# Conditioning beside every second piece in the first layer and every piece in the second; the feed-forward's first products in one matmul of 512 columns and one of 256

## The reference, cut to what matters

```
def swiglu(x, w1, w3, w2):
    return (jax.nn.silu(x @ w1) * (x @ w3)) @ w2        # 1024 -> 2816 -> 1024
...
for i in range(DEPTH):                                  # two layers
    x = layer_norm(DEEPNORM_ALPHA * x + mix, ln1_g[i], ln1_b[i])
    x = layer_norm(DEEPNORM_ALPHA * x + swiglu(x, ffn_w1[i], ffn_w3[i], ffn_w2[i]), ln2_g[i], ln2_b[i])
    x = x + jax.nn.sigmoid(x @ ple_w_gate[i] + ple_b_gate[i]) * (p[i] @ ple_w_proj[i])
...
mod = jax.nn.silu(c) @ w_ada[l] + b_ada[l]              # second block: 1024 -> 6144, once
```

## Time and profile before

| | |
|---|---|
| median of 3 runs | 1837.02 us (1832.55 to 1837.19) |
| the profiled execution | 1836.56 us |
| its span, first to last instruction | 1835.0 us |
| PE busy | 1768.0 us (96%) |
| DVE busy | 1245.4 us (68%) |
| ACT busy | 902.1 us (49%) |
| read from memory | 172 GB/s over the span |

### The profile page before, as it was taken

One profiled execution on the slowest core, in us unless ns is written; L12 is line 12 of the kernel. 1 busy time (PEld: TensorE's weight loads), 2 busy tenths in 40 slices (PEclk: granted clock), 3 DMA queues, 4 the chain that ended last, 5 costly groups with the idle time before them and its releaser, 6 DMA issues.

```text
span 1835.0 us, 32435 instructions
## 1 busy us (share of the span) xinstructions
PE 1768.0 (96%) x11628; PEld 1593.5 (87%) x11628; DVE 1245.4 (68%) x2324; ACT 902.1 (49%) x1585; POOL 206.8 (11%) x148
## 2 busy tenths in 40 slices
PE   9999999799999999998989999999999999999997
PEld 8769998678879997796779999999998998888886
DVE  5467767776768666856656884777886556666666
ACT  5634443355544433646335545777774444333333
POOL 1010000001110000021112788000000000000000
PEclk9999999899999999998989999999999999999999
DMA  7424658745536666344214455444345555555553
GB/s 241 173 98 155 251 181 298 249 168 173 168 113 226 233 235 223 127 154 138 75 64 152 159 184 182 144 144 141 139 139 172 183 184 182 192 186 190 188 188 133
DMA packets 86359, 317.60 MB, mean 173 GB/s; under 512 B 9632, under 2 KB 9904, under 8 KB 85488
## 3 DMA queue, kind: packets, MB, share of 16 engines
q1 hardware_dynamic: 77328, 279.48, 43.7%
q10 hardware_dynamic: 7200, 25.45, 4.0%
q0 software_dynamic: 1728, 11.25, 1.7%
HBM read 315.08 MB, written 1.05 MB: 172 GB/s over the span
## 4 chain that ended last, share of the span: by engine, by line
PE 70%; DVE 4%; ACT 2%; issue 1%; POOL 0%; ACTq 0%; DVEq 0%; POOLq 0%
PE bank L244 21%; PE bank L246 21%; PE bank L245 21%; PE bank L2202 3%; ACT wh L192 1%; DVE wl L199 1%; PE bank L489 1%; PE bank L524 1%; PE bank L559 0%; PE bank L2046 0%; PE bank L523 0%; PE bank L490 0%; DVE ss_s L527 0%; DVE xl L368 0%; PE bank L342 0%
## 5 line engine op out<-in xcount | busy, mean ns | idle before, releaser
L192 ACT ACTIVATE wh<-ring 128x1024 fp32r<-128x1024 f32 x529 | 559.3, 1059 | 776.0 <-PE bank L246 708.4
L199 DVE TENSOR_TENSOR wl<-ring,wh 128x1024 fp32r<-128x1024 f32 x479 | 586.4, 1226 | 440.0 <-ACT wh L192 440.0
L244 PE MATMUL bank<-xh,wh 128*128 128x256 f32 x2072 | 597.2, 288 | 6.8 <-DVE xl L368 6.6
L246 PE MATMUL bank<-xh,wl 128*128 128x256 f32 x2072 | 589.4, 284 | 0.0
L245 PE MATMUL bank<-xl,wh 128*128 128x256 f32 x2072 | 589.1, 284 | 0.0
L244 PEld LDWEIGHTS bank<-xh,wh 128*128 128x128 f32 x2072 | 400.5, 193 | 10.4 <-issue 7.7
L245 PEld LDWEIGHTS bank<-xl,wh 128*128 128x128 f32 x2072 | 400.0, 193 | 1.1
L246 PEld LDWEIGHTS bank<-xh,wl 128*128 128x128 f32 x2072 | 399.8, 193 | 0.0
L244 PE MATMUL bank<-wh,wa_high 128*128 128x512 f32 x512 | 202.4, 395 | 2.1 <-DVE weighted L2221 1.4
L246 PE MATMUL bank<-wh,wa_low 128*128 128x512 f32 x512 | 201.9, 394 | 0.0
L245 PE MATMUL bank<-wl,wa_high 128*128 128x512 f32 x512 | 201.9, 394 | 0.0
(11 more groups left out here) (431 smaller groups left out, 2235.3 us busy)
## 6 DMA issues: line engine op xcount, KB each, us to landing
ring<-in_stream SPq DMA_DIRECT2D x529, 512.0 KB, 3.3
ada<-in_w_ada ACTq DMA_DIRECT2D x48, 512.0 KB, 4.5
rows<-in_rows POOLq DMA_DIRECT2D x1, 2560.0 KB, 12.5
rows<-in_rows POOLq DMA_DIRECT2D x2, 1024.0 KB, 5.2
con<-in_early POOLq DMA_DIRECT2D x1, 1374.0 KB, 15.2
x_feature_major<-in_x_fm SPq DMA_DIRECT2D x4, 256.0 KB, 5.2
x<-in_x_tm POOLq DMA_DIRECT2D x1, 1024.0 KB, 5.6
weighted<-in_subkeys POOLq DMA_DIRECT2D x1, 1024.0 KB, 5.3
```

The source lines that it names most:

```text
L192: C.activation(wh[q % AHEAD][:, :], ring[slot][:, :], ACT.Copy).then_inc(s_high, 1)
L199: low.tensor_tensor(wl[q % AHEAD][:, :], ring[slot][:, :], wh[q % AHEAD][:, :], ALU.subtract).then_inc(s_low, 1)
L244: T.matmul(o, left[0], right[0], start=start, stop=False, skip_group_check=True)
L246: return T.matmul(o, left[1], right[0], start=False, stop=stop, skip_group_check=True)
```

## The change

`xh` and `xl` become halves of one tensor `xs`, in which both halves of a k stand side by side, 2 x 256 columns. A first product's step over k is then one matmul that streams all 512 columns past `wh` (sums of the high half in a bank's first 256 columns, of the low half in the other 256) and one that streams 256 past `wl`. The two halves of the bank must be added afterwards: an ACT copy and a DVE add for `ga` and the same for `gb`. `ada["every"]` behind the first products is 2 in layer 0 and 1 in layer 1, where it was 1 in both.

```diff
-    xh = sb(base, "xh", [P, KD, S], F32R)
-    xl = sb(base, "xl", [P, KD, S], F32R)
+    xs = sb(base, "xs", [P, KD, 2, S], F32R)
+    xh, xl = xs[:, :, 0, :], xs[:, :, 1, :]
...
+        def wide(g, k, h, l):
+            ks = slice(k * P, (k + 1) * P)
+            T.matmul(g[:, :], h[:, ks], xs[:, k, :, :].rearrange("p a t -> p (a t)"), start=k == 0, stop=False,
+                     skip_group_check=True)
+            return T.matmul(g[:, 0:S], l[:, ks], xh[:, k, :], start=False, stop=k == KD - 1, skip_group_check=True)
...
-                        last = mm3(g[:, 0:S], (h[:, k * P:(k + 1) * P], l[:, k * P:(k + 1) * P]),
-                                   (xh[:, k, :], xl[:, k, :]), k == 0, k == KD - 1)
+                        last = wide(g, k, h, l)
...
-                    C.activation(sg[u % 3][:, :], ga[:, 0:S], ACT.Silu).then_inc(s_silu, 1)
-            V.wait_ge(s_used, s + (q + 2))
-            V.wait_ge(s_silu, n3 + (u + 1))
-            V.tensor_tensor(hf[u % 3][:, :], sg[u % 3][:, :], gb[:, 0:S], ALU.mult).then_inc(s_gate, 1)
+                    C.activation(sg[u % 3][:, :], ga[:, S:2 * S], ACT.Copy).then_inc(s_silu, 1)
+                    V.wait_ge(s_silu, n9 + (3 * u + 1))
+                    V.tensor_tensor(sg[u % 3][:, :], ga[:, 0:S], sg[u % 3][:, :], ALU.add).then_inc(s_gate, 1)
+            C.wait_ge(s_gate, n15 + (5 * u + 1))
+            C.activation(sg[u % 3][:, :], sg[u % 3][:, :], ACT.Silu).then_inc(s_silu, 1)
+            C.wait_ge(s_used, s + (q + 2))
+            if i is not None or u >= 3:
+                C.wait_ge(s_gate, n15 + 5 * (u - 3) + 5)
+            C.activation(hf[u % 3][:, :], gb[:, S:2 * S], ACT.Copy).then_inc(s_silu, 1)
+            V.wait_ge(s_silu, n9 + (3 * u + 3))
+            V.tensor_tensor(hf[u % 3][:, :], gb[:, 0:S], hf[u % 3][:, :], ALU.add).then_inc(s_gate, 1)
+            V.wait_ge(s_gate, n15 + (5 * u + 2))
+            V.tensor_tensor(hf[u % 3][:, :], sg[u % 3][:, :], hf[u % 3][:, :], ALU.mult).then_inc(s_gate, 1)
...
-        ada["every"] = 1
+        ada["every"] = 2 - layer
         y = project((hh, hl), KF, sums[0:2], need=gated_in)
```

More of the change, by code:

```diff
@@ L1076, in products_side_by_side @@
                     h, l = wh[(q0 + piece) % AHEAD], wl[(q0 + piece) % AHEAD]
-                    last = mm3(bank[3 * piece][:, 0:S], (h[:, k * P:(k + 1) * P], l[:, k * P:(k + 1) * P]),
-                               (xh[:, k, :], xl[:, k, :]), k == 0, k == KD - 1)
+                    last = wide(bank[3 * piece], k, h, l)
                     if k == KD - 1:
@@ L1084, in tile @@
             n3 = 0 if i is None else i * 3
+            n9 = 0 if i is None else i * 9
+            n15 = 0 if i is None else i * 15
             s = 0 if i is None else i * BODY
@@ L1091, in tile @@
                     if i is not None or u >= 3:
-                        T.wait_ge(s_gate, 3 * n3 + 3 * (u - 3) + 1 if i is not None else 3 * (u - 3) + 1)
+                        T.wait_ge(s_gate, n15 + 5 * (u - 3) + 2)
                 def products(h, l, g=g):
@@ L1108, in tile @@
                     if i is not None or u >= 3:
-                        C.wait_ge(s_gate, 3 * n3 + 3 * (u - 3) + 1)
-                    C.activation(sg[u % 3][:, :], ga[:, 0:S], ACT.Silu).then_inc(s_silu, 1)
-            V.wait_ge(s_used, s + (q + 2))
-            V.wait_ge(s_silu, n3 + (u + 1))
-            V.tensor_tensor(hf[u % 3][:, :], sg[u % 3][:, :], gb[:, 0:S], ALU.mult).then_inc(s_gate, 1)
-            V.wait_ge(s_gate, 3 * n3 + (3 * u + 1))
+                        C.wait_ge(s_gate, n15 + 5 * (u - 3) + 3)
+                    C.activation(sg[u % 3][:, :], ga[:, S:2 * S], ACT.Copy).then_inc(s_silu, 1)
[11 more added lines that the diff above has]
+            V.tensor_tensor(hf[u % 3][:, :], sg[u % 3][:, :], hf[u % 3][:, :], ALU.mult).then_inc(s_gate, 1)
+            V.wait_ge(s_gate, n15 + (5 * u + 3))
             row = u if i is None else bass.ds(n3 + u, 1)
@@ L1118, in tile @@
             V.tensor_copy(hrow, hf[u % 3][:, :]).then_inc(s_gate, 1)
-            V.wait_ge(s_gate, 3 * n3 + (3 * u + 2))
+            V.wait_ge(s_gate, n15 + (5 * u + 4))
             V.tensor_tensor(lrow, hf[u % 3][:, :], hrow, ALU.subtract).then_inc(s_gate, 1)
@@ L1155, in ffn @@
         sums = [bank[6], bank[7], bank[1], bank[4]]
-        gated_in = lambda k: pe.wait((s_gate, 3 * max(k + 1, KF - 2)))
-        ada["every"] = 1
+        gated_in = lambda k: pe.wait((s_gate, 5 * max(k + 1, KF - 2)))
+        ada["every"] = 2 - layer
         y = project((hh, hl), KF, sums[0:2], need=gated_in)
@@ L1705, in opened @@
         pe.wait(zr)
-        T.matmul(bank[4][:, :], zrow[:, :], xh[0:1, 0:2, :].rearrange("p a t -> p (a t)"), start=True, stop=False,
+        T.matmul(bank[4][:, :], zrow[:, :], xs[0:1, 0, :, :].rearrange("p a t -> p (a t)"), start=True, stop=False,
                  skip_group_check=True)
```

1 line of the change is left out of this document (removed).

## The result

| | before | after |
|---|---|---|
| median | 1836.78 us (1832.55 to 1838.79, 8 runs) | 1842.39 us (1834.25 to 1848.32, 8 runs) |
| profiled execution | 1836.56 us | 1840.76 us |

The ratio is 1.0033, 95% interval 1.0021 to 1.0045: slower by 0.33%. The forecast was no change, 1836 us; the time lies within its range.

A forecast was written before the change was run, and what follows sets the result against it. PE, busy for 96% of the span, was taken as the bound. The profiled 1836.6 us, less 9.2 (first products), less 14.4 (layer 0), plus 23.1 (layer 1), gave 1836.1 us; range for 8 in 10: 1828 to 1845.

The forecast's parts named there:

- The first products: PE's k-steps in both layers' first products: 0.360 to 0.347 us over 704 steps, 9.2 us gained, at the least 4.2.
- The sum: All terms added to the profiled execution: 1836.6 less 9.2, less 14.4, plus 23.1, giving 1836.1 us.
- DVE and ACT: First products' extra copies and adds: costed at nothing, ACT having room and three pieces of lead covering DVE's tight tiles.
- Layer 0: Behind layer 0's first products, half the conditioning steps: 6.15, 4.9 and 3.3 us gained, together 14.4.
- Layer 1: Behind layer 1's first products, 11 more conditioning steps left for later: 1.3 + 20.1 + 1.7 = 23.1 us lost (21 to 29).
- the row: Eight leftover conditioning steps after layer 1's residual, ahead of the low half PE needs: eighth starts at 15.8 us, ends at 17.0.
- the 1.3 us of loss ahead of it: Layer 1's first `project`, a step at each of 11 steps: PE runs dry after 40.7 us where pieces take 39.4.
- The clock's part: PE coming back slow after layer 1's idle stretch: 1.7 us added (none, or 3.4).
- The rival that layer 1 keeps its lead: Layer 1's row begins over 3 us earlier with three pieces ready, PE idles some 13 us for 20.1: 1828; chance 0.22.
- DVE as the bound: Rival in the first products: waits make a loop tile 5.9 us on DVE, 44 tiles lose 15 us: 1851; chance 0.12.
- Halving: Rival that layer 0's halved steps still fall behind, half of the 14.4 us stays: 1843; chance 0.16 with the 512-column pace.
- The second part of that rival: First products' 512-column pace is 0.234 us or more, giving 1841; chance 0.16 together with layer 0's halving.

The follow-up runs named there:

- e1: The changed kernel with the conditioning as before, so only the wide first products; 1829.8 us, ratio to before 0.9965.
- e6: e1 with the 512-column operand placed behind the buffers of the pieces in SBUF instead of before them; 1829.8 us, ratio to before 0.9964.
- e7: e1 with the low-weights matmul first in each k-step from the second on; 1829.1 us, ratio to before 0.9966.
- e8: e1 with two more DVE instructions in every tile, writing a buffer nobody reads; 1834.5 us, ratio to before 0.9995.
- e2: The kernel before with only the conditioning's new places, first products as before; 1843.7 us, ratio to before 1.0043.
- e11: e1 with one more matmul of 64 columns at the start of each piece, its sums overwritten; 1839.4 us in one run.

## Why the prediction was wrong

**The first products: the step that failed.** "I take 9.2" was the term that was mis-sized. The sum took 0.347 us for every k-step, and the reason given, that twelve 512-column matmuls in a row agreed with it, was a poor one: those stream a piece past weights of `xh`, and have no 256 between them. In the first profiled execution the k-steps outside the half-clock stretches took 0.353, which is the lower bound of 4.2 us that the prediction had worked out and not taken. With it the prediction's own sum is 1836.6 - 4.2 - 14.4 + 23.1 = 1841.1 us; the execution took 1840.8. The measured terms are 4.4, 15.1 and 24.2 us, which make 4.7 us more; the span grew by 4.5. The median stands 5.6 us above before, just past the 0.3% that was called no change. The runs put this in the place of the step: the gain is 9.2 or 4.2 us or between, by the pace that each stage happens to have, and e1, e6 and e7 measured 6.2 to 6.6 us (0.34 to 0.36%) in the median. That 0.347 is the fast pace is in part luck: it was put together from 0.227 and 0.120 us, and the fast pace's matmuls take 0.232 and 0.115.

The Trainium skill, "TensorE: Matmul & The Clock Gate", section "Back-to-back issue gap", gives a single matmul at full clock the columns divided by 2.4 GHz plus 2.5 ns, by which the pair is an estimate of 0.325 us. The traces do not agree: both paces stand above it, by 22 and 28 ns.

**The sum: a second step that failed in the median.** The terms were added as if they did not touch each other. By the ratios the wide matmuls alone gained 6.4 us for the 9.2, 2.8 short, and the conditioning alone lost 7.9 us for the 8.7 forecast. Together they should be 1.5 us slower than before; the changed kernel is 6.1 and 8.4 us slower. The 4.6 to 7.0 us that come only with both are more than the pace took, and they stood in the sum at nothing. In the profiled executions 2.8 us of it is the longer idle stretch of layer 1 with what surrounds it; the rest lies, as far as the traces show, in where half clock falls. The cause stays open.

**DVE and ACT: right.** A queued tile took 5.5 us on DVE, and PE never waited for a low half there. The two copies took 0.37 us each and the adds 0.42, as bounded; the loop tile is 4.15 us for the forecast 4.4. That the cover is thin was right too: e8 broke it with 0.67 us a tile, in tiles with `x_block` or a conditioning step (2, 3 and 8) and in those next behind them (4, 5 and 9 to 12).

**Layer 0: right.** 14.4 forecast; measured 6.0 in the second products, 4.7 to the first product behind the layer norm, 4.4 by the 4.15 us stall that is gone: 15.1 us. e2 shows the same without the wide matmuls.

**Layer 1: right in size, and in mechanism but for one engine.** 23.1 forecast, 24.2 measured. The working had only DVE's list behind the row; ACT's stood behind it too, and its high halves came at 705.70 us, still ahead of DVE's turn, so that the size did not suffer. The idle stretch was forecast at 20.1 and was 20.3 us. The row was a little longer than in the working (16.5 us from its first step's start to its last's, for 15.8), and the 1.3 us of loss ahead of it came as a 0.92 us stall. The clock's part was taken at 1.7 and was 2.6 us (5.18 at half clock). The rival that layer 1 keeps its lead fell: the row began at 692.07, 41.7 us after the stage's start, with nothing left to PE at 691.23.

**The other rivals.** DVE as the bound did not appear; the loop tile has 1.4 us of room, and e8 had to add 0.67 us a tile to make the tiles beside `x_block` and the conditioning steps longer. Halving did all it said. The second part of that rival, a 512-column pace of 0.234 us or more giving 1841 us, is what came: 0.237 in the mean of the slow pattern. It stood in the text with too small a chance, although every kind of 512-column matmul in the trace of before but the one with `xh` as weights stood at 0.231 to 0.235 in the median.

## What to carry to other kernels

A background job's leftovers must not be worked off in a row ahead of an instruction that the busiest engine needs: eight steps cost 24 us in a row, and 9 beside the pieces behind them. Look at every engine whose list the row stands in, here ACT's as well as DVE's. Spread such steps thinly (here stages that moved 264 and 278 GB/s had no stall, those that moved 310 and 311 had), and count what halving in one place pushes into another. Where large terms cancel, the verdict hangs on the smallest: take its pace from rows with the same operands on both sides, or keep both bounds as cases, and leave room for what only the parts together show.

## What the runs showed of the hardware that was not expected

- The alternation of a 512- and a 256-column matmul runs at one of two steady paces, 0.3467 or 0.3533 us for the pair, in one and the same program; one execution of the changed kernel had the fast one in layer 0 and the slow one in layer 1. The fast pace repeats every two pairs, the slow one every three. With a disturbance in each piece both came in a fixed order (e7, e11). With two of each width side by side it was 0.348 in both layers of both executions.
- In idle stretches of PE of 19.5 and 20.3 us the granted clock fell (0.56 and 0.62 on average over them), and PE then worked at half clock, 1.2 GHz, for another 3.4 and 5.2 us.
- Conditioning loads under way two at a time, with almost nothing else moving, took 3.2 us in the median in a row of eight and 4.3 us in a row of twelve.
